# A chunked recurrence whose state passes between 64-token halves of a unit

## What is computed

```python
def wkv7(r, w, k, v, a, b):
    # S_t = S_{t-1} diag(w_t) + (S_{t-1} a_t) b_t^T + v_t k_t^T ;  y_t = S_t r_t
    s0 = jnp.zeros((B, H, N, N), jnp.float32)
    def step(S, inp):
        r_t, w_t, k_t, v_t, a_t, b_t = inp
        sa = jnp.einsum('bhvk,bhk->bhv', S, a_t)
        S = S * w_t[:, :, None, :] + sa[..., None] * b_t[:, :, None, :] + v_t[..., None] * k_t[:, :, None, :]
        y = jnp.einsum('bhvk,bhk->bhv', S, r_t)
        return S, y
...
y = wkv7(rh, wh, kh, vh, -kk, kk * ah)
# then a group norm by head, its gain and bias, + sum(r * k * r_k) * v, times g (a gate), @ wo
```

## Time and profile before

| | us |
|---|---|
| median of 3 runs | 1394.4 (1393.77 to 1394.46) |
| span of the profiled execution | 1392.2 |
| TensorE busy | 1362.8 (98%) |
| VectorE busy | 855.2 (61%) |
| ScalarE busy | 696.6 (50%) |
| GpSimd busy | 38.1 (3%) |
| seven rounds and the first pairs, 780.90 to 880.44 and on to 895.72 | 114.8 |
| from there to the transposes of token block 1, 922.30 | 26.6 |

### The profile page before, as it was taken

The page is one execution under the profiler, slowest core; times in us unless marked ns, Lnnn a source line. Parts: engine busy times, 40 slices in busy tenths (PEclk is TensorE's granted clock), DMA queues, the critical chain, the costliest instruction groups (busy, mean ns, idle before and its releaser), DMA issues.

```text
span 1392.2 us, 23783 instructions
## 1 busy us (share of the span) xinstructions
PE 1362.8 (98%) x8927; PEld 1117.8 (80%) x8927; DVE 855.2 (61%) x1234; ACT 696.6 (50%) x1110; POOL 38.1 (3%) x42
## 2 busy tenths in 40 slices
PE   8999999999999999999999999999999999999998
PEld 7888877778888878888787688778888887788887
DVE  4545577875755464445784788766555677555554
ACT  5444456675465464444554444235444566644442
POOL 0000000000000000000001000110000010000000
PEclk9999999999999999999999999999999999999999
DMA  8655545556444565555352101314555651265552
GB/s 294 214 181 181 181 140 202 167 188 200 161 163 157 148 207 197 189 195 186 115 196 77 61 4 33 112 46 166 181 189 184 227 175 52 83 212 194 182 184 104
DMA packets 145537, 220.25 MB, mean 158 GB/s; under 512 B 16761, under 2 KB 65295, under 8 KB 145329
## 3 DMA queue, kind: packets, MB, share of 16 engines
q1 hardware_dynamic: 145456, 219.14, 47.8%
HBM read 218.04 MB, written 1.05 MB: 157 GB/s over the span
## 4 chain that ended last, share of the span: by engine, by line
PE 88%; DVE 6%; ACT 3%; issue 1%; POOL 1%; DMA 1%; SPq 0%; DVEq 0%; ACTq 0%; POOLq 0%
PE acc L291 12%; PE acc L293 12%; PE gp L291 12%; PE acc L292 12%; PE gp L293 12%; PE gp L292 12%; PE tp L944 1%; PE gp L2767 1%; PE acc L2782 1%; DVE sb_w_lo L280 1%; PE acc L1280 1%; PE tp L291 1%; ACT sb_w_hi L264 1%; ACT sb_arena L407 1%; DMA sb_raw<-in_ffn_w 1%
## 5 line engine op out<-in xcount | busy, mean ns | idle before, releaser
L280 DVE TENSOR_TENSOR sb_w_lo<-sb_raw,sb_w_hi 128x1024 fp32r<-128x1024 f32 (+1 forms) x380 | 451.5, 1214 | 207.4 <-ACT sb_w_hi L264 205.7
L264 ACT ACTIVATE sb_w_hi<-sb_raw 128x1024 fp32r<-128x1024 f32 (+1 forms) x380 | 387.9, 1052 | 210.9 <-PE acc L293 106.9
L291 PE MATMUL gp<-sb_w_hi,sb_xa_hi 128*128 128x512 f32 (+1 forms) x752 | 298.5, 397 | 5.0 <-DVE sb_w_lo L280 3.5
L293 PE MATMUL gp<-sb_w_lo,sb_xa_hi 128*128 128x512 f32 (+1 forms) x752 | 291.7, 388 | 0.0
L292 PE MATMUL gp<-sb_w_hi,sb_xa_lo 128*128 128x512 f32 (+1 forms) x752 | 291.2, 387 | 0.0
L291 PEld LDWEIGHTS gp<-sb_w_hi,sb_xa_hi 128*128 128x128 f32 x752 | 141.3, 188 | 37.8 <-DVE sb_w_lo L280 6.7
L293 PEld LDWEIGHTS gp<-sb_w_lo,sb_xa_hi 128*128 128x128 f32 x752 | 141.2, 188 | 29.6
L292 PEld LDWEIGHTS gp<-sb_w_hi,sb_xa_lo 128*128 128x128 f32 x752 | 141.5, 188 | 27.1 <-issue 0.5
L291 PE MATMUL acc<-sb_w_hi,sb_mid_hi 128*128 128x512 f32 x400 | 156.2, 390 | 0.0
L293 PE MATMUL acc<-sb_w_lo,sb_mid_hi 128*128 128x512 f32 x400 | 155.8, 390 | 0.0
L292 PE MATMUL acc<-sb_w_hi,sb_mid_lo 128*128 128x512 f32 x400 | 155.7, 389 | 0.0
(11 more groups left out here) (417 smaller groups left out, 1756.8 us busy)
## 6 DMA issues: line engine op xcount, KB each, us to landing
sb_raw<-in_ffn_w SPq DMA_DIRECT2D x264, 256.0 KB, 4.3
sb_raw<-in_mlp_w SPq DMA_DIRECT2D x256, 256.0 KB, 2.9
sb_raw<-in_w_in SPq DMA_DIRECT2D x72, 256.0 KB, 3.2
sb_raw<-in_a_w_rkv SPq DMA_DIRECT2D x48, 256.0 KB, 4.1
sb_raw<-in_xattn_w_kv SPq DMA_DIRECT2D x32, 256.0 KB, 3.6
sb_raw<-in_w_out SPq DMA_DIRECT2D x16, 256.0 KB, 3.2
sb_raw<-in_xattn_w_q SPq DMA_DIRECT2D x16, 256.0 KB, 3.1
sb_raw<-in_xattn_w_o SPq DMA_DIRECT2D x16, 256.0 KB, 3.1
```

The lines of the kernel that those rows point to most:

```text
L264: A.e.activation(w_hi[:, s, :, 0:n], raw[:, r, :, 0:n], ACT.Copy).then_inc(hi_done, 1)
L280: V.e.tensor_tensor(w_lo[:, s, :, 0:n], raw[:, r, :, 0:n], w_hi[:, s, :, 0:n].bitcast(F32), ALU.subtract).then_inc(lo_done, 1)
L291: e.matmul(dst, xh, wh, start=start, stop=False)
L293: return e.matmul(dst, xh, wl, start=False, stop=stop)
```

## The change

- `pe_pairs` no longer forms the blocks below the diagonal: 16 matmuls of 64x64 weights over 128 columns replace 8 of 64x128 over 256. The masks are two operations, not four; `first_x` is one, not two.
- The columns come in two halves (`pe_columns(u, j)`), each through one bank, and the second waits for the copy of the first. The first ones wait for another exponential.
- `pe_values` multiplies values with keys, 128 columns of weights at a time, once for the right-hand side and for y. `pe_from_state` adds what the state gives to both, for the odd half in every unit and for the even half where t = 1.
- The carry is gone, with its addition on VectorE. The state after the even half is formed inside the unit (`pe_k_state`, `pe_b_state`, `dve_state` by half) and the odd half reads it. `pe_y` has only the u part left.
- The right-hand side and y are each copied by ScalarE in two copies of 64 partitions.
- The gates of token block 1 move from `pe_out` to before the last `pe_y`.
- Constants in DRAM are 513 columns fewer.

```diff
-            def pe_columns(self, T, u):
+            def pe_columns(self, T, u, j):
                 s, i, t, g = self.place(u)
...
+                T.e.wait_ge(self.rows_ready, t + 1)
+                if j:
+                    T.e.wait_ge(self.cols, 2 * u + 1)
+                elif i:
+                    T.e.wait_ge(self.inv_y_done[s], LEVELS * i)
                 else:
...
+                    T.e.wait_ge(self.exp_c, s + 1)
+                out = self.bank_a(s)
+                T.e.transpose(out.rearrange("p (b s) -> p b s", b=8)[:, 0:4:3, :], self.pair_rows(4, t, g, j), ident)
+                T.e.transpose(out[:, HALF:HALF + P], self.pair_rows(7, t, g, j), ident)
+                T.e.transpose(out[:, 256:256 + P], self.pair_rows(2, t, g, j), ident)
+                T.e.transpose(out[:, 384:384 + P], self.pair_rows(5, t, g, j), ident).then_inc(*T.one(self.turned))
             def pe_pairs(self, T, u):
...
                 fm = self.fm[i % 2][s]
                 T.e.wait_ge(self.cols, 2 * (u + 1))
                 if i:
-                    T.e.wait_ge(self.state_done, min(u - 1, self.GROUPS))
+                    T.e.wait_ge(self.u_done, 2 * (u - 1))
                 for j in range(2):
-                    if i and j:
+                    if j and i:
                         T.e.wait_ge(self.y_done, u - 1)
...
+                        T.e.wait_ge(self.state_done, self.states(u - 2, 1))
+                    elif j:
+                        T.e.wait_ge(self.prev_exp, NT)
+                        T.e.wait_ge(*stage(self.taken, 11 + s))
+                    for k in range(2):
+                        for par in range(2):
+                            at = COLUMN_TILES[par]
+                            for e in range(2):
+                                part = COLUMN_TILES[e]
+                                dst = self.pair_bank(s, j)[at, e, k * P:(k + 1) * P]
+                                mm = T.e.matmul(dst, fm[part, j, 4 + 2 * k + par, :], fm[part, j, 2 * par:2 * par + 2, :].rearrange("p b s -> p (b s)"),
+                                                start=True, stop=True)
+                    mm.then_inc(*T.one(self.pairs))
...
-            def pe_rhs(self, T, u):
+            def pe_values(self, T, u, n):
                 s, i, t, g = self.place(u)
...
+                if n:
+                    T.e.wait_ge(self.values, self.values_made(u, 0))
+                elif i:
+                    T.e.wait_ge(self.y_done, u - 1)
                 for j in range(2):
...
+                    for par in range(2):
+                        e = par if n == 0 else 1 - par
+                        at = COLUMN_TILES[par]
+                        mm = T.e.matmul(self.bank_of(s, e)[:, self.place_in(par, j)], self.mt[s][at, e, j, 1, :], self.head_rows(6, t, g, 2 * j + e)[at],
+                                        start=n == 0 and j == 0, stop=True, skip_group_check=True)
+                mm.then_inc(*T.one(self.rhs if n and t == 0 else self.values))
+            def pe_from_state(self, T, u, par):
+                s, i, t, g = self.place(u)
+                if par:
+                    T.e.wait_ge(self.state_done, self.states(u, 0))
+                else:
+                    T.e.wait_ge(self.values, self.values_made(u, 1))
+                    T.e.wait_ge(self.state_done, self.states(u - self.GROUPS, 1))
+                for j in range(2):
+                    for e in range(2):
+                        part = COLUMN_TILES[e]
+                        mm = T.e.matmul(self.bank_of(s, e)[:, self.place_in(par, j)],
+                                        self.fm[i % 2][s][part, j, 2 * par:2 * par + 2, :].rearrange("p b s -> p (b s)"), self.s_buf[part, 2 * g + j, :],
+                                        start=False, stop=True, skip_group_check=True)
                 mm.then_inc(*T.one(self.rhs))
...
+            def pe_k_state(self, T, u, par, m):
+                s, i, t, g = self.place(u)
+                j, e, at = m // 2, m % 2, COLUMN_TILES[par]
+                T.e.matmul(self.bank_of(s, par)[COLUMN_TILES[e], j * HALF:(j + 1) * HALF], self.head_rows(5, t, g, m)[at], self.head_rows(6, t, g, m)[at],
+                           start=False, stop=False, skip_group_check=True)
+            def pe_b_state(self, T, u, par, m):
+                s, i, t, g = self.place(u)
+                j, e, at = m // 2, m % 2, COLUMN_TILES[par]
+                mm = T.e.matmul(self.bank_of(s, par)[COLUMN_TILES[e], j * HALF:(j + 1) * HALF], self.head_rows(2, t, g, m)[at], self.u_buf[s][at, m, :],
+                                start=False, stop=True, skip_group_check=True)
+                if m == 3:
+                    mm.then_inc(*T.one(self.state))
...
+            def pe_u_even(self, T, u):
                 s, i, t, g = self.place(u)
                 T.e.wait_ge(self.inv_y_done[s], LEVELS * (i + 1))
-                T.e.wait_ge(self.rhs_done, u + 1)
+                T.e.wait_ge(self.rhs_done, 2 * u + 1)
                 for m in range(4):
...
+                    self.pe_k_state(T, u, 0, m)
+                    self.pe_u(T, u, 0, m)
+            def pe_state_even(self, T, u):
                 T.e.wait_ge(self.u_done, 2 * u + 1)
                 for m in range(4):
...
+                    if u < self.GROUPS:
+                        self.pe_k_state(T, u, 1, m)
+                    self.pe_b_state(T, u, 0, m)
+            def pe_u_odd(self, T, u):
+                T.e.wait_ge(self.rhs_done, 2 * u + 2)
                 for m in range(4):
...
+                    self.pe_u(T, u, 1, m)
+            def pe_state_odd(self, T, u):
+                T.e.wait_ge(self.u_done, 2 * u + 2)
+                for m in range(4):
+                    self.pe_b_state(T, u, 1, m)
             def pe_y(self, T, u):
                 s, i, t, g = self.place(u)
                 T.e.wait_ge(self.u_done, 2 * u + 2)
                 if t == 0:
...
+                    T.e.wait_ge(self.state_done, self.states(u, 1))
                 for j in range(2):
...
+                    for e in range(2):
+                        for par in range(2):
+                            at = COLUMN_TILES[par]
+                            mm = T.e.matmul(self.bank_of(s, e)[at, self.place_in(par, j)], self.mt[s][at, e, j, 0, self.r_columns(par)],
+                                            self.u_buf[s][at, 2 * j + e, :], start=False, stop=True, skip_group_check=True)
                 mm.then_inc(*T.one(self.y))
...
                 for u in range(1, self.UNITS):
+                    w = u - 1
                     self.pe_pairs(T, u)
...
+                    self.pe_z(T, w, 3)
                     self.pe_a_mat(T, u)
-                    self.pe_xy(T, u - 1, 3)
+                    self.pe_values(T, w, 0)
+                    self.pe_xy(T, w, 3)
+                    self.pe_values(T, w, 1)
                     self.pe_z(T, u, 0)
-                    self.pe_z(T, u - 1, 4)
+                    self.pe_z(T, w, 4)
                     self.pe_xy(T, u, 0)
-                    self.pe_xy(T, u - 1, 4)
+                    if w >= self.GROUPS:
+                        self.pe_from_state(T, w, 0)
+                    self.pe_xy(T, w, 4)
                     self.pe_z(T, u, 1)
-                    self.pe_u_first(T, u - 1)
+                    self.pe_u_even(T, w)
                     self.pe_xy(T, u, 1)
-                    self.pe_carry(T, u - 1)
+                    self.pe_state_even(T, w)
                     self.pe_z(T, u, 2)
+                    self.pe_from_state(T, w, 1)
                     if u + 1 < self.UNITS:
...
+                        self.pe_columns(T, u + 1, 0)
+                    self.pe_u_odd(T, w)
+                    if u + 1 < self.UNITS:
+                        self.pe_columns(T, u + 1, 1)
+                    if w < self.GROUPS:
+                        self.pe_state_odd(T, w)
                     self.pe_xy(T, u, 2)
-                    self.pe_y(T, u - 1)
+                    self.pe_y(T, w)
                 last = self.UNITS - 1
                 y = rows(7)[:, 0, :]
                 self.pe_z(T, last, 3)
+                self.pe_values(T, last, 0)
                 T.e.wait_ge(self.g2_loaded, 64)
                 T.e.wait_ge(self.y_done, last)
                 self.pe_gate(T, 0, 0)
                 self.pe_xy(T, last, 3)
+                self.pe_values(T, last, 1)
                 self.pe_gate(T, 0, 1)
                 self.pe_z(T, last, 4)
                 self.turn.pe_wide(T, 0, 0, self.spare_bank(0), y, (self.y_rows, 1))
+                self.pe_from_state(T, last, 0)
                 self.pe_xy(T, last, 4)
                 self.turn.pe_wide(T, 0, 1, self.spare_bank(1), y, (self.y_rows, 2))
-                self.pe_rhs(T, last)
                 self.pe_out_part(T, 0, 0, range(0, 1))
-                self.pe_u_first(T, last)
+                self.pe_u_even(T, last)
                 self.pe_out_part(T, 0, 0, range(1, 2))
-                self.pe_carry(T, last)
```

(46 more changed lines are left out.)

## The result

| | before | changed |
|---|---|---|
| median us (runs) | 1394.43 (4) | 1406.15 (4: 1402.57, 1405.08, 1407.23, 1409.71) |
| ratio, 95% interval | | 1.0083 (1.0071 to 1.0094) |
| span of the profiled execution | 1392.2 | 1400.8 |
| mean granted clock of each run | 1.000 in the profiled one | 0.989 to 0.995 |

The changed kernel is 0.83% slower, 9 us above the forecast and 5.6 above the upper end of the range. The busy times on its page, to be laid beside the earlier trace rows: TensorE has 128 more matmul instructions and, within 1 us, the same busy time.

What follows compares the result with a forecast made beforehand. TensorE, 98% busy, was taken to bound the kernel, as a written queue of small matmuls with short waits. 1392.2 − 1.9 (head and rounds) + 4.6 (tail) + 2.2 (profile to median) = 1397.1 us; range 1389.8 to 1400.5.

Steps and rivals of the forecast that it cites:

- The walk of the rounds and the head: Start of the stage and its seven rounds: −1.9 us summed to the last unit's z, with −1.6 from the head.
- The stall on y: Rounds' start: second pairs wait for the previous unit's y copy, beginning at 0.92 instead of 0.48; new stall of 0.45 us.
- the halved pairs: Pair matmuls take 0.96 us instead of 1.93, four tiles at a time; in the head this gives 0.5 us.
- the later z in round 6: Round 6: z of level 0 at 5.77 us instead of 5.03; with from_state, +1.1 for the round.
- the four-block rounds: Rounds 5 to 7, with four 128-column blocks, not three: −0.3, +1.1 and −0.2 us.
- the weight split: ScalarE's 1.05 us split in rounds 1 to 3 delays y's copy by 0.6; rounds 2 to 4 become 14.38, +0.1 together.
- The 128-column tile: values and from_state: loading 128 weight columns binds at 0.11 us a step, 0.53 for a four-step block.
- the rival of hidden loads: values and from_state: weight loads run beside matmuls, four-step blocks take 0.3 us, total 1391.9; chance 0.22.
- The tail: Last unit's z to second transpose: 25.05 up to y's end plus a 6.1 chain, 31.15 against 26.58 us, +4.6.
- the −0.57: Tail chain behind the last y: 0.57 us saved since the first gate product no longer waits for its gate.
- The clock: Rival: the tail's new TensorE idle time lowers the clock, +1.4 us, total 1398.5; chance 0.12.
- the slow ones: Slower rivals: clock falls in the tail, 1398.5, chance 0.12; pair tiles run two at a time, 1400.5, chance 0.08.

Runs made afterwards that it cites:

- e12: The kernel before with only the 12 weight loads of 256 KB held back one round, from round 7 to the tail; median 1393.48 us.
- e5: Changed kernel with gates back behind the last y, shift and scaling behind the masks, y's copy ahead of the weight split on ScalarE; median 1403.08 us.
- e8: e5 with the 12 weight loads of 256 KB held back one round, from round 7 to the tail; median 1394.01 us.
- e1: Changed kernel with the four gate matmuls of token block 1 back behind the last y; median 1399.51 us, ratio 1.0039.
- e3: Changed kernel with unread extra matmuls, 1.05 us each, in three waits: before a_mat of round 7 and both transposes of token block 1; median 1406.95 us.
- e7: Changed kernel with unread 0.53 us matmuls in four waits: before a_mat of round 7, first output matmuls and both transposes; median 1402.68 us.
- e11: Changed kernel with only the 12 weight loads held back one round; median 1408.35 us.
- e2: Changed kernel with VectorE's shift of round 5 and group norm scaling of round 6 behind the next round's masks and first x; median 1406.36 us.
- e10: Changed kernel: gates behind last y, shift and scaling behind masks, 12 weight loads a round later, group norm's two loads a round apart; 1394.11 us.
- e14: e10 with the group norm's two loads together again; median 1392.95 us, ratio 0.9990 to the kernel before.
- e15: e14 with 4 unread extra matmuls of 256 columns in the tail's 2.17 us wait; median 1391.73 us, ratio 0.9981 to the kernel before.

## Why the prediction was wrong

- **The walk of the rounds and the head** was right in its mechanisms: −1.9 at the last unit's z forecast, −2.15 at a full clock. That the sum fits so well is in part luck, since its terms miss by −0.3 (head), −0.4 (rounds 2 to 4), +0.1, +0.2 and +0.2 (rounds 1, 5 and 7). The stall on y, the halved pairs (0.49 from the first to the second in the head), the later z in round 6 and the four-block rounds are in the trace. The stall was sized wrongly both ways: the second pairs begin 1.17 after the first in rounds 5 to 7, where 0.9 was forecast, and 1.35 in rounds 2 to 4, where the weight split was to make it 1.5.
- **The 128-column tile**: 0.59 for a block of four steps, 0.53 forecast; the rival of hidden loads, 0.3, is refuted, and with it 1391.9 (24 blocks at 0.53 − 0.3 = 0.23, not 0.21, would even have been 1391.4). The low end of the range rested on it.
- **The tail**: +5.3 against +4.6. The work up to y's end fits (25.2; the terms named for the 25.05 add up to 24.96), the chain behind it is 6.65, not 6.1. The failed term is the −0.57 for a first gate product that no longer waits for its gate. The idle time of VectorE before it was 0.60 and is 0.46, in all 14 versions of the changed kernel, wherever the gates stand; only in e6, the old kernel with its gates ahead, is it 0.10. In all 14 it starts as ScalarE's square ends (925.25 here), but no semaphore of the square is waited for, and in e6 the two overlap; what holds it is not shown. The other 0.1 is in y's two copies (0.78 against 0.38). Rows of VectorE:

```profile
881.78 1.22 DVE L3331 TENSOR_TENSOR sb_arena<-sb_arena,sb_stat 128x1024 f32<-128x1024 f32 x1 [1.44 <-POOL sb_stat L3367]
882.92 0.68 DVE L3122 TENSOR_TENSOR sb_shade<-acc,sb_consts 128x512 f32<-128x512 f32 x1
...
925.26 0.69 DVE L3361 TENSOR_TENSOR sb_arena<-sb_arena,gt 128x512 f32<-128x512 f32 x1 [0.46 <-DVE sb_arena L3311]
```

  The last row is the gate product. The first two show why TensorE waited 1.66 in round 7: VectorE waits for GpSimd's power, does the scaling behind it, and only then the mask that a_mat needs.
- **The clock** is the step that failed. The sum had it at nothing; the rival priced one fall, at one place, +1.4, with a chance of 0.12. The fall behind the transposes measured +1.40. But the clock fell also in round 7 (+2.63), where the sum had no more than the length of the wait, and in the first transformer block (+1.62), and in other executions elsewhere: 19 us at half rate per run. Fits of time against half-rate time over the runs of each experiment give 0.25 to 0.6 us for each of them (e12, with hardly any, left out); the falls of the profile gave 0.4 to 0.5. The rows to see it with were there: TensorE waited 0.51 for the masks in round 6 already, which grows when work goes from under them, and 1.51 in the tail. I asked of one new idle stretch what it does to the clock, and of the others only what they cost in time.
- **Instructions.** The kernel before has this row in round 7, and I passed over it since it was short:

```profile
890.81 0.21 PE L2782 MATMUL acc<-sb_shadow 64*64 64x64 f32 x1 [0.57 <-issue]
```

  Nothing in the prediction has this mechanism. The runs show it by the packets and by e5 against e8. The changed kernel's own profile has no such wait of 0.48 us or more; that its three slower executions had any is inferred from e1, e3, e7 and e11, whose round 5 has the same queue of TensorE. Why the changed kernel is hit oftener is not settled: it executes 256 more instructions in the stage (128 matmuls with their loads), and its rounds are 0.1 us shorter, both small beside the 3.3 to 7 us from one packet to the next. It may be only the place of the packets against the bursts; in e2, e10, e14 and e15 TensorE waited 0.8 to 1.1 us in that place, and never long. That was argued, not tried.
- **Range.** It took in each mechanism once, added to none of the others. Of the slow ones only the clock came, but at several places in one execution.

The falls inside and near the stage by the wait of TensorE at which they began, over all profiles: the wait of 2.72 us where it stood unfilled, 5 of 5; waits for instructions of 2.25 to 2.7 us, 6 of 6; 2.17 in the tail, 7 of 10; 1.66 in round 7, 3 of 4; 1.39 to 1.44 in round 6, 2 of 4 (in a third, a fall began 2.4 us behind it); 1.51 in the tail of the old order, 0 of 3; 1.65 before the first transpose, 0 of 4; the 9 places filled with matmuls, none (two were the place of 2.72, two that of 1.66, three that of 2.17). So falls come at the long waits and went where these were filled: chance alone is refuted. But the length of a wait does not decide by itself. A wait of 1.39 us near 1170 us, in all 17 profiles, never had a fall, and the one in the first transformer block began some 1.2 us behind a wait of 0.63. What else counts is open. The Trainium skill, page "TensorE: Matmul & The Clock Gate", Part 1, says that the half clock is the default to which an idle array returns; by that rule, these runs agree, and they show besides that the same wait gives a fall in one execution and none in another. The Trainium skill, page "Runtime: NRT & Kernel Launch", Instruction fetch mechanics, says that an engine's sequencer fetches blocks of 256 instructions over a DMA queue of its own and that this is mostly hidden; the packets agree, but beside loads in bursts it was not hidden here: TensorE waited up to 2.68 us.

## What to carry to other kernels

Where TensorE is 98% busy, ask of every edit that opens a wait on it of over a microsecond what the clock does behind it. Read the granted clock by stretches and not the busy share, and fill such a wait or put back what covered it: here a block of gates moved ahead of the chain that it had covered cost 3.5 us in the chain and about 3 more, mostly clock. In stretches of small matmuls try holding large loads back a round, since instruction packets came late beside them here; an "issue" wait of half a microsecond in the profile is the warning. Holding them back paid 1 us in the old kernel and 7 to 9 in e5, and nothing where the other waits stayed (e11). Before an operation is moved ahead of another on an engine (y's copy, the shift), look up whose copy stands behind it and what load it waits for.

## What the runs showed of the hardware

- A wait of TensorE for its own instructions beside a load burst: 2.25 to 2.68 us in six profiles, and VectorE, ScalarE and GpSimd idle with it in e1; without a burst none was longer than 0.50.
- Instruction packets of 16 KB, one in 3.3 to 7 us in this stage where none is late and the clock is full, each 0.9 to 1.6 us long; a wait ends 2.2 to 2.9 us behind a packet's start.
- The clock at half for 3.4, 6.8, 10.2, 13.7 or 23.9 us at a time, with TensorE listed as busy all through; a fall of 3.4 us cost 1.40 and 1.62 us, one of 6.8 cost 2.63. With 19 instead of 1.5 us at half rate the spread of the runs is wider, 7.1 us (4 of the changed kernel) against 4.3 (82 of the kernel before, 1393.47 to 1397.76).
- 64-row weights of 128 columns with 64 streamed columns: 0.11 us a step, as for one streamed column with 128 rows.
- An fp32 copy by ScalarE of 64 partitions and 256 columns takes as long as one of 128 partitions: two take 0.78 us, one of 128 took 0.38.
